# First attention regrouped by head with one masked row minimum, and adjacent columns for the compression's matmuls

## What is computed

```python
def causal_block_attention(q, k, v):      # first block, 8 heads, q and k 96 wide, v 64 wide
    ...
        s = jnp.einsum('bqhd,bkhd->bhqk', qblk, k).astype(jnp.float32) * scale
        mask = kpos[None, :] <= qpos[:, None]
        s = jnp.where(mask[None, None], s, -jnp.inf)
        p = jax.nn.softmax(s, axis=-1).astype(v.dtype)
        return jnp.einsum('bhqk,bkhd->bqhd', p, v)
```

```python
def compress(kv_raw, pe, w1, w2):
    idx = jnp.arange(n_cmp)[:, None] * D_CMP + jnp.arange(L_CMP)[None, :]
    blocks = kv_raw[:, idx] + pe[None, None, :, None, :]
    blocks = blocks.transpose(0, 1, 3, 2, 4).reshape(bsz, n_cmp, N_KV_GROUPS, L_CMP * HEAD_DIM)
    return jax.nn.silu(blocks @ w1) @ w2
```

## Time and profile before

| | |
|---|---|
| median of 3 runs | 2948.09 us (2946.34 to 2950.89) |
| the profiled execution | 2953.82 us, its span 2952.0 us |
| PE busy over the span | 2836.4 us (96%) |
| DVE, ACT, POOL busy | 1821.5, 1007.6, 1012.7 us |
| stage `mla`, from its first matmul to the last flush | 125.8 to 264.3 us |
| compression matmuls of `nsain` | 2213.3 to 2227.9 and 2252.5 to 2267.1 us |

### The profile page before, as it was taken

The page is one execution under the profiler, slowest core; times in us unless marked ns, Lnnn a source line. Parts: engine busy times, 40 slices in busy tenths (PEclk is TensorE's granted clock), DMA queues, the critical chain, the costliest instruction groups (busy, mean ns, idle before and its releaser), DMA issues. The chain is left out here.

```text
span 2952.0 us, 38732 instructions
## 1 busy us (share of the span) xinstructions
PE 2836.4 (96%) x14624; PEld 2519.5 (85%) x14624; DVE 1821.5 (62%) x3378; ACT 1007.6 (34%) x1603; POOL 1012.7 (34%) x630
## 2 busy tenths in 40 slices
PE   8897999999999999999999999999999799899998
PEld 7655799999999999999998787888878698778886
DVE  5775787988888587888887753332051688343311
ACT  4355233444434322222223323222232478222221
POOL 3412400221213242334332644444432255344442
PEclk9997999999999999999999999999999799999999
DMA  3101256796969998989995232333332100233332
GB/s 129 40 1 47 91 145 219 237 288 198 321 181 342 326 330 312 322 321 330 328 324 182 85 101 79 100 99 96 98 121 81 32 1 1 79 93 100 98 99 68
DMA packets 195641, 475.76 MB, mean 161 GB/s; under 512 B 17280, under 2 KB 103936, under 8 KB 193152
## 3 DMA queue, kind: packets, MB, share of 16 engines
q1 hardware_dynamic: 114000, 343.24, 35.7%
q0 software_dynamic: 27648, 100.68, 9.8%
q10 hardware_dynamic: 53808, 29.36, 3.3%
HBM read 415.45 MB, written 56.62 MB: 160 GB/s over the span
## 5 line engine op out<-in xcount | busy, mean ns | idle before, releaser
L264 ACT ACTIVATE w_hi<-w 128x1024 fp32r<-128x1024 f32 (+2 forms) x485 | 506.3, 1046 | 1237.6 <-DVE ffn_gates L2157 324.4
L274 POOL TENSOR_TENSOR w_lo<-w,w_hi 128x1024 fp32r<-128x1024 f32 (+2 forms) x229 | 539.9, 2368 | 731.6 <-ACT w_hi L264 731.6
L274 DVE TENSOR_TENSOR w_lo<-w,w_hi 128x1024 fp32r<-128x1024 f32 x256 | 313.5, 1224 | 151.3 <-ACT w_hi L264 121.5
L309 PE MATMUL peer_psum<-xn_hi,w_hi 128*128 128x416 f32 x1024 | 365.9, 357 | 0.0
L1487 POOL DMA_INDIRECT peer_gathered<-in_peer_u,peer_chosen_here x96 | 152.4, 1588 | 614.2 <-DVEq L1742 483.8
L309 PE MATMUL peer_psum<-peer_w_hi,w_hi 128*128 128x416 f32 x1024 | 360.0, 352 | 2.5 <-DVE peer_w_lo L406 1.8
L310 PE MATMUL peer_psum<-xn_lo,w_hi 128*128 128x416 f32 x1024 | 361.0, 353 | 0.0
L311 PE MATMUL peer_psum<-xn_hi,w_lo 128*128 128x416 f32 x1024 | 360.7, 352 | 0.0
L310 PE MATMUL peer_psum<-peer_w_lo,w_hi 128*128 128x416 f32 x1024 | 359.2, 351 | 0.0
L311 PE MATMUL peer_psum<-peer_w_hi,w_lo 128*128 128x416 f32 x1024 | 359.1, 351 | 0.0
L309 PE MATMUL ffn_psum<-ffn_hn_hi,w_hi 128*128 128x512 f32 x704 | 276.0, 392 | 10.4 <-DVE ffn_hn_lo L619 6.6
(11 more groups left out here) (411 smaller groups left out, 5529.0 us busy)
## 6 DMA issues: line engine op xcount, KB each, us to landing
w<-in_peer_uT SPq DMA_DIRECT2D x128, 512.0 KB, 4.3
w<-in_peer_v SPq DMA_DIRECT2D x128, 512.0 KB, 5.4
w<-in_f_w_gu SPq DMA_DIRECT2D x88, 512.0 KB, 3.7
peer_act<-peer_act_out SPq DMA_DIRECT2D x128, 208.0 KB, 5.3
peer_gate<-peer_gates_out ACTq DMA_DIRECT2D x26, 1024.0 KB, 8.6
peer_gates<-peer_gate SPq DMA_DIRECT2D x16, 1664.0 KB, 9.5
peer_act_in<-peer_act SPq DMA_DIRECT2D x128, 208.0 KB, 4.5
w<-in_f_w_down SPq DMA_DIRECT2D x32, 512.0 KB, 3.5
```

What stands on the lines that cost most here:

```text
L264: act.activation(self.hi[:, x, 0:c], self.buf[:, x, 0:c], ACT.Copy).then_inc(self.rounded, 1)
L274: eng.tensor_tensor(self.lo[:, x, 0:c], self.buf[:, x, 0:c], self.hi[:, x, 0:c].bitcast(F32), ALU.subtract).then_inc(self.split, 1)
L309: pe.matmul(out, w[0], x[0], start=start, stop=False)
```

## The change

In `mla` the items go head by head (four query tiles of head 0, then head 1). Each query tile has one fixed place in PSUM for its scores (`ROW_AT`), so four rows are kept instead of two. The scores of query tiles 0 and 1 of a head are issued together. Where the 16 meta keys and the rest fit one bank, one matmul does both. The mask is a row of 400 zeros with the triangle at its end, written once by POOL and ACT, and one DVE operation adds it and takes the row's minimum. Probabilities have 8 rows; they and the diagonals (now 31, one for each tap, without waits) lie where the normalised input lay. Transposes are grouped by key tile, for all queries that see it (`KEY_TILES`), six steps behind the scores, into two PSUM banks. The products with the values follow seven steps behind: one matmul for each key tile over all its queries. ACT makes one copy for each group (32 in place of 64), and flushes each head (8 half-height copies in place of 4). The loop is 39 steps long on PE, 35 before. In `nsain` the dimensions of X are in another order; PE's 124 columns are now four runs of 31 adjacent numbers, and DVE's writes step 512 bytes.

```diff
+TURN_BEHIND, SUM_BEHIND = 6, 7
+ROW_AT = (0, NMETA + P, 512, 1536 - NMETA)
+KEY_TILES = (((0, 0), (0, 1), (0, 2), (0, 3)), ((ST, 0), (ST, 1), (ST, 2), (ST, 3)), ((1, 1), (1, 2), (1, 3)),
+             ((2, 2), (2, 3), (3, 3)))
...
+    def score(self, pe, n):
+        h, j = n // ST, n % ST
+        if n >= ST and j != 1:
+            pe.wait_ge(self.s["exped"], max(n - ST + 1, ST * (h - 1) + 2))
+        row, q = self.row(n), self.q[:, h, j * P:(j + 1) * P]
+        for a, b in ((0, NMETA), (NMETA, T1)) if j == ST - 1 else ((0, row.shape[-1]),):
+            mm = pe.matmul(row[:, a:b], q, self.k[:, h, a:b], start=True, stop=True)
+        mm.then_inc(self.s["scored"], 1)
+
+    def turn(self, pe, u):
+        h = u // ST
+        if u % ST == 0:
+            pe.wait_ge(self.s["scaled"], ST * (h + 1))
+        if u >= len(self.PT):
+            pe.wait_ge(self.s["copied"], u - len(self.PT) + 1)
...
+    def add(self, pe, u):
+        h = u // ST
+        pe.wait_ge(self.s["copied"], u + 1)
+        if u % ST == 0 and h >= 2:
+            pe.wait_ge(self.s["flushed"], h - 1)
...
+    def on_pe(self, pe, between, ahead):
+        for n in range(self.n_items + SUM_BEHIND):
+            if n < self.n_items:
+                for m in ((n, n + 1), (), (n,), (n,))[n % ST]:
+                    self.score(pe, m)
+            ahead(n)
+            if TURN_BEHIND <= n < self.n_items + TURN_BEHIND:
+                self.turn(pe, n - TURN_BEHIND)
+            if SUM_BEHIND <= n:
+                self.add(pe, n - SUM_BEHIND)
+            between(n)
...
+                    dve.tensor_tensor_reduce(out=row, in0=row, in1=self.wide[:, T1 - row.shape[-1]:], scale=1.0, scalar=3e38,
+                                             op0=ALU.add, op1=ALU.min, accum_out=self.nm[:, m % 4:m % 4 + 1])\
+                       .then_inc(s["maxed"], 1)
...
+                pool.memset(at.wide[:, 0:T1 - P], 0.0).then_inc(at.s["mask_made"], 1)
                 for k in range(CK):
-                    if k >= DIAGS:
-                        pool.wait_ge(diag_used, k - DIAGS + 1)
-                    pool.tensor_scalar(diag[:, k % DIAGS, :], kit.ident[:, :], kit.gain("conv_w", k * CT + on_tensor), None,
-                                       ALU.mult).then_inc(diag_made, 1)
...
-        X = nc.alloc_sbuf_tensor_at("nsain_X", [P, 2, 2, NG, SEQ // DC, DC // 2], F32, offset=io["q2_at"])
+        X = nc.alloc_sbuf_tensor_at("nsain_X", [P, 2, 2, DC // 2, NG, SEQ // DC], F32, offset=io["q2_at"])
...
-                                           X[:, kind, win, :, win:win + NC, r], start=(m == 0), stop=(m == LC // 2 - 1))
+                                           X[:, kind, win, r, :, win:win + NC], start=(m == 0), stop=(m == LC // 2 - 1))
...
-                                X[:, kind, win, g, :, :], raw[:, g, :].rearrange("p (n r) -> p n r", r=DC)[:, :, 0:DC:2],
+                                X[:, kind, win, :, g, :].rearrange("p r n -> p n r"),
+                                raw[:, g, :].rearrange("p (n r) -> p n r", r=DC)[:, :, 0:DC:2],
```

More of the change, by code:

```diff
@@ L942, in _ @@
                 own.wait()
[L946 to L1025, removed]
@@ L1050, in on_act @@
-            for b, i in self.last.items():
-                if i + self.lag + 1 == n:
-                    act.wait_ge(s["summed"], i + 1)
-                    self.flush(act, b, self.O[b % len(self.O)]).then_inc(s["flushed"], 1)
-            if between is not None:
-                between(n)
-    extra = 0
-    def on_dve(self, dve, between=None):
-        it, s, n_items = self.items, self.s, len(self.items)
-        own = Count(dve, s["steps"])
-        back = self.lag - 1
-        for n in range(n_items + self.lag + 3):
-            m = n - back
-            if n < n_items:
-                x = it[n]
-                S = self.S[n % len(self.S)]
-                dve.wait_ge(s["scored"], n + 1)
-                col, mask = x["mask"]
-                own.step(dve.tensor_tensor(S[:, col:col + mask.shape[-1]], S[:, col:col + mask.shape[-1]], mask,
-                                           ALU.add))
-                masked = own.n
-            if 0 <= m < n_items:
+            u = n - TURN_BEHIND
@@ new lines, in on_act @@
+            if 0 <= u < self.n_items:
+                act.wait_ge(s["turned"], u + 1)
+                if u >= 3:
+                    act.wait_ge(s["summed"], u - 2)
+                tiles = KEY_TILES[u % ST]
+                w, c = (P if tiles[0][0] < ST else NMETA), len(tiles) * P
+                act.activation(self.pts[0:w, u % 3, 0:c], self.PT[u % len(self.PT)][0:w, 0:c], ACT.Copy)\
+                   .then_inc(s["copied"], 1)
+            u = n - SUM_BEHIND - 1
+            if u >= 0 and u % ST == ST - 1:
+                act.wait_ge(s["summed"], u + 1)
+                self.flush(act, u // ST, self.O).then_inc(s["flushed"], 1)
@@ new lines, in on_act, with on_dve @@
+            between(n)
+    def on_dve(self, dve, between):
+        s = self.s
+        dve.wait_ge(s["mask_made"], 2)
+        for n in range(self.n_items + SUM_BEHIND + 2):
+            if n < self.n_items:
+                for m in ((n, n + 1), (), (n,), (n,))[n % ST]:
+                    row = self.row(m)
+                    dve.wait_ge(s["scored"], max(m + 1, ST * (m // ST) + 2))
+                    dve.tensor_tensor_reduce(out=row, in0=row, in1=self.wide[:, T1 - row.shape[-1]:], scale=1.0, scalar=3e38,
+                                             op0=ALU.add, op1=ALU.min, accum_out=self.nm[:, m % 4:m % 4 + 1])\
+                       .then_inc(s["maxed"], 1)
+            if 0 <= n - 1 < self.n_items:
+                m = n - 1
```

109 lines of the change are left out of this document (58 added, 51 removed).

## The result

The changed kernel takes 2924.1 us (median of four runs, 2920.1 to 2930.7); the kernel before takes 2949.5 in the same comparison. The ratio is 0.991, with a 95% interval of 0.9898 to 0.9921: some 25 us faster. The forecast was 2928, within 2917 to 2938. The profiled execution took 2924.65 us, the forecast for it 2934.0, so its gain was 29 us and not 20.

A forecast was written before the change was run, and what follows sets the result against it. PE, busy 2836.4 of 2952.0 us, was taken to bound the kernel. Compression 12.8, attention's first part 5 and second part 2 sum to 19.8 us off the 2948.1 median, giving 2928 us, range 2917 to 2938.

The forecast's parts named there:

- What bounds the kernel: Whole kernel: PE busy 2836.4 of 2952.0 us; savings in the two touched stages count in full, since stages end in barriers.
- First compression: First block in `nsain`, full clock: adjacent columns cut a record from 0.229 to 0.115 us, saving 7.3 us.
- Second: Second compression in `nsain`: 3.5 us at clock 0.50, where some 16 records gain nothing and 48 gain; saving 5.5 us.
- upper bound of 15 us: Both compressions in `nsain` together: the saving if there is no cold spell; forecast 12.8 us, lower bound 11.
- DVE's side: DVE's writes of X in `nsain`: 512-byte steps add 0.4 us each, hidden by a slack of 0.65 us per operation.
- rival D: Writes of X: DVE's 512-byte steps far dearer, kernel slower, from 3.5 us per operation; 2956 us at 4.5; chance 0.03.
- First part of the attention: `mla`, steps 0 to 16: DVE becomes the limit; 1.5 us from the mask plus 3.9 from waits, about 5 us saved.
- Second part: `mla`, step 17 to the last flush: fewer ACT copies and looser coupling against a longer tail; 2 us saved, bounds -6 and +8.
- rival B: Attention gains 16 us: scores four items ahead halve ACT's 24.3 us of waiting, PE stays warm; 2919 us; chance 0.12.
- The tail: End of `mla`: last head's 14 transposes and 5 products, about 1.5 + 3.0 us at full clock, twice that at the lower.
- A: Attention gains nothing: PE and ACT stay chained, early gain spent on deferred work and cold tail; 2935 us; chance 0.21.
- C: Compression's pace is not the address step, so only the attention counts; 2941 us; chance 0.09.

The follow-up runs named there:

- run with column steps: Changed kernel with X's columns 8 bytes apart in the first compression, 16 in the second, DVE writing smaller pieces; 0.116 and 0.23 us a record.
- runs of one half each: Kernel before with X's new order alone: 2940.98 us, ratio 0.9962; changed kernel with X's old order, so the attention's half: 2940.14 us, 0.996.

## Why the prediction was right, and where not

**What bounds the kernel.** Right: both places paid their full length, since PE works without a pause around the compression and a barrier ends `mla`. 28.2 of 29.2 us lie in them.

**First compression.** 7.3 us forecast, 7.36 measured. **Second.** 5.5 forecast; 5.65 in the run with the layout alone, 7.28 in the changed kernel, whose clock did not fall after the same pause. The working was right; that the fall of the earlier trace rows would come again was a chance and not a step of the sum. The upper bound of 15 us had it.

**DVE's side.** +0.4 us per operation forecast: 3.91 us for the first eight (0.49 each, +0.15), 6.12 for the second, timeline of DVE:

```profile
2175.14 3.91 DVE L2395 TENSOR_TENSOR nsain_X<-nsain_raw,nsain_pe 128x256 f32<-128x256 f32 x8
2185.18 6.12 DVE L2395 TENSOR_TENSOR nsain_X<-nsain_raw,nsain_pe 128x256 f32<-128x256 f32 x8
```

In the run with the layout alone the two times are 3.90 and 6.12 us. Seven of the second eight cost what the first did. One took 2.79 us, and the timeline of both engines shows why: it started inside an operation of GpSimd on the weights and ended 0.49 us, the length of one such write, after it.

```profile
2187.58 2.79 DVE L2395 TENSOR_TENSOR nsain_X<-nsain_raw,nsain_pe 128x256 f32<-128x256 f32 x1
...
2187.27 2.61 POOL L274 TENSOR_TENSOR w_lo<-w,w_hi 128x1024 fp32r<-128x1024 f32 x1 [3.05 <-ACT w_hi L264]
```

The run with the layout alone has the same pair (2201.70 us, 2.79; 2201.38 us, 2.61). In the run with column steps it was GpSimd's operation that stretched, to 3.99 us from the usual 2.40, beside DVE's smaller writes. So 2.3 us of the 6.12 are this meeting and not the layout's price; the forecast had no such term, and PE was not held up by it. The first compression starts on time, so the cover held and rival D with it fell; it would have taken 3.5 us per operation.

**First part of the attention.** 5 us forecast, 6.9 measured. The last taps start at 182.70 us and end at 185.8 (186.5 forecast), the mean comes at 190.27 (192). DVE became the limit, as said, and its waits for scores inside the steps fell from 3.9 to 2.3 us (9.7 less the 7.4 at the barrier), not to none. Counted from the first matmul, the last taps end 5.6 us sooner (66.1 and 60.5 us), near the forecast. The other 1.3 us fall between the last taps and the mean, a stretch for which the forecast had no term: DVE waited there 1.49 us for a score before, 0.23 after.

```profile
193.96 0.30 DVE L1070 TENSOR_TENSOR mla_psum<-mla_psum,tri 128x128 f32<-128x128 f32 x1 [1.49 <-PE mla_psum L983]
```

Inside the 5.6 us two terms were mis-sized in opposite directions. The fused mask was put at 0.08 us per item, 1.5 us in all; the mask and minimum of a row of 528 took 0.70 us to the next tap and not 0.87, so it saves 0.25 us per item against the old form. The 0.60 + 0.14 us of the earlier trace rows were a sum of two durations that overlap with what follows. The waits were to give 3.9 us and gave 1.6. That the sum came out near is in part luck. Also too simple: PE's saved records were said to count only as long as PE paces. They are worth 1.9 us in a part in which DVE paces.

**Second part.** 2 us forecast, 6.7 measured; this is the larger miss. The working of this term names neither of the two small savings. Taking back the fused mask costs 3.3 us here and taking back the joined scores 2.3, together 5.6 of 6.7 us (or some 4.7, with the dearer form of the mask counted off). Each item goes from PE to DVE to ACT, and both savings lie between two hands, so the idle time of the engines did not hide them. What the term named instead, fewer copies and rarer handing over, is the order, and that alone is worth 0.3 to 1.2 us. The 1.3 us less on ACT did not come here: ACT was busy 41.15 us before and 42.40 after, and what it saved lies in the first part (32.99 and 29.12 us, from the windows of each part). ACT's wait for minima fell from 24.3 to 12.5 us, as rival B had it, whose total (2919 for the median, 16 us in the attention) was nearer to the profiled 13.6 than the forecast's 7; but B's reason, scores four items ahead, is refuted by the run with the scores held back. That the product would still wait for the copy one step before was right: 17.0 us and 16.9. The tail was only half as cold as feared: windows of 3 us of PE in the changed kernel have 0.56 from 241 us and 1.00 from 247, where the last products run, for which the forecast had named the lower clock.

```profile
241.00:244.00 3.00, 3.00 (x10) 0.56 0.03 5
244.00:247.00 3.00, 3.00 (x13) 0.88 0.00 0
247.00:250.00 3.00, 2.45 (x11) 1.00 0.01 3
```

**The rivals.** A and C fell with the runs of one half each (ratios 0.996 and 0.9962, both intervals below 1), D with DVE's times. The median lies 3.9 us under the forecast and the profiled execution 9.4; the latter is the plainer comparison with the terms, and its misses are 1.8 us (compression), 1.9 and 4.7 us (attention), and 1 in stages that nobody touched. All four lie on one side; the median looks better because the profiled execution before lay 5.7 us over its median, the one after only 0.5.

## What to carry to other kernels

Where work goes from engine to engine, count a saving on a step between two of them, even if every engine has idle time (3.3 and 2.3 us here; in the old order the fused mask gave 1.4 us in the same part, so it need not count in full). Where two engines are near their limit, expect a saving on one of them to show little until the other is relieved too (the fused mask in the first part: at most 0.6 us in the old order, some 1.2 to 3.7 when taken out of the new one). Before a difference of 1 to 3 us between two executions is put down to an instruction, compare the granted clock of both, window by window. Take the cost of an instruction as the distance from its start to the start of the next, not as a sum of durations. Before a layout is turned over to make a moving operand adjacent, see whether half of it does: columns 8 bytes apart ran as fast here.

## What the runs showed of the hardware

- A matmul record of 124 float32 columns costs 0.114 us with its moving columns 4 bytes apart (64 in 7.30 us), 0.116 at 8 bytes (7.42), 0.23 at 16 (14.44) and at 32 (14.66). At 16 and 32 bytes the pace was the same at both levels of the granted clock.
- The clock after a pause is not settled by the stage's program: with the same instructions and the same pause of PE (1.8 us before the second compression, 3.0 us in the attention) it fell to 0.50 in one execution and stayed at 1.00 in another. Two such falls cost 1.6 and 2.9 us, about the size of the effects that were looked for.
- DVE's writes with a step of 512 bytes cost 0.49 us for 256 elements a row, where they cost 0.34 with the 256 side by side.
- A DVE addition of two SBUF operands that began inside a GpSimd operation on SBUF did not end before it: 2.79 us, of which the last 0.49 came after GpSimd's end (two kernels). In a third, GpSimd's operation took 3.99 us in place of 2.40 beside DVE's.
